# Sparse attention in a two-block kernel: the scores of two heads issued in turn, and two sets of buffers for the turned probabilities

## The reference, cut to what matters

```python
s_s = einsum('bqghd,bgqkd->bghqk', q_b, k_g) + bias_s      # selected
o_s = einsum('bghqk,bgqkd->bqghd', masked_softmax(s_s, mask_s), v_g)
s_w = einsum('bqghd,bkgd->bghqk', q_b, k_w) + head_bias(dist_w)   # window
o_w = einsum('bghqk,bkgd->bqghd', masked_softmax(s_w, mask_w), v_w)
return g_b[..., 0:1] * o_c + g_b[..., 1:2] * o_s + g_b[..., 2:3] * o_w
```

## Time and profile before

| | us |
|---|---|
| median of three runs | 2572.99 (2572.43 to 2579.61) |
| the profiled execution, its own time | 2573.83 |
| its span in the trace | 2572.1 |
| the stage `attend` in it, 2232.3 to 2335.4 | 103.1 |

### The profile page before, as it was taken

One profiled execution on the slowest core, in us unless ns is written; L12 is line 12 of the kernel. 1 busy time (PEld: TensorE's weight loads), 2 busy tenths in 40 slices (PEclk: granted clock), 3 DMA queues, 4 the chain that ended last, 5 costly groups with the idle time before them and its releaser, 6 DMA issues. The chain is left out here.

```text
span 2572.1 us, 38698 instructions
## 1 busy us (share of the span) xinstructions
PE 2339.2 (91%) x15386; PEld 2132.0 (83%) x15386; DVE 1557.1 (61%) x2843; ACT 1131.4 (44%) x1962; POOL 75.0 (3%) x36
## 2 busy tenths in 40 slices
PE   6976779789999999999998998989998999897998
PEld 6964468689999998888887997979997999776997
DVE  5764343479988887666665545665545544565454
ACT  4521233435555444555554444444433443454443
POOL 0121000040100000000000000000000000000000
PEclk9987589899999999999998998999998999788999
DMA  5450033325544444656655555535545554103552
GB/s 202 147 61 10 20 142 117 128 103 173 172 149 148 148 149 148 196 192 194 195 173 199 183 182 197 197 115 211 182 163 200 213 193 166 70 1 118 209 181 98
DMA packets 77854, 388.55 MB, mean 151 GB/s; under 512 B 9707, under 2 KB 12651, under 8 KB 49292
## 3 DMA queue, kind: packets, MB, share of 16 engines
q1 hardware_dynamic: 76380, 382.08, 43.1%
q0 software_dynamic: 1040, 4.19, 1.6%
q10 hardware_dynamic: 288, 0.26, 0.0%
HBM read 381.26 MB, written 5.24 MB: 150 GB/s over the span
## 5 line engine op out<-in xcount | busy, mean ns | idle before, releaser
L243 DVE TENSOR_TENSOR split_slots<-ring,split_slots 128x1024 fp32r<-128x1024 f32 x394 | 464.2, 1224 | 355.3 <-ACT split_slots L234 355.3
L296 PE MATMUL banks<-x_transposed_hi,split_slots 128*128 128x256 f32 x2016 | 581.3, 288 | 44.6 <-PEq L355 39.9
L297 PE MATMUL banks<-x_transposed_lo,split_slots 128*128 128x256 f32 x2016 | 578.9, 287 | 0.0
L298 PE MATMUL banks<-x_transposed_hi,split_slots 128*128 128x256 f32 x2016 | 578.2, 287 | 0.0
L234 ACT ACTIVATE split_slots<-ring 128x1024 fp32r<-128x1024 f32 x404 | 402.5, 1049 | 257.3 <-PE banks L298 224.4
L307 DVE SCALAR_TENSOR_TENSOR expert_lo<-ring,expert_hi 128x512 fp32r<-128x512 f32 x512 | 360.7, 710 | 189.0 <-ACT expert_hi L302 187.9
L302 ACT ACTIVATE expert_hi<-ring 128x512 fp32r<-128x512 f32 x512 | 323.2, 632 | 276.0 <-PE banks L298 275.9
L296 PEld LDWEIGHTS banks<-x_transposed_hi,split_slots 128*128 128x128 f32 x2016 | 395.5, 196 | 49.7 <-issue 42.9
L297 PEld LDWEIGHTS banks<-x_transposed_lo,split_slots 128*128 128x128 f32 x2016 | 395.3, 196 | 1.5
L298 PEld LDWEIGHTS banks<-x_transposed_hi,split_slots 128*128 128x128 f32 x2016 | 395.0, 196 | 0.0
L296 PE MATMUL banks<-x_transposed_hi,expert_hi 128*128 128x256 f32 x1024 | 296.3, 289 | 17.7 <-DVE expert_lo L307 17.2
(11 more groups left out here) (444 smaller groups left out, 3480.8 us busy)
## 6 DMA issues: line engine op xcount, KB each, us to landing
ring<-in_ffn_w SPq DMA_DIRECT2D x132, 1024.0 KB, 4.8
ring<-in_peer_u SPq DMA_DIRECT2D x128, 512.0 KB, 3.3
ring<-in_peer_v SPq DMA_DIRECT2D x128, 512.0 KB, 4.3
ring<-in_w_in SPq DMA_DIRECT2D x16, 1024.0 KB, 4.9
ring<-in_sgu_w_in SPq DMA_DIRECT2D x16, 1024.0 KB, 4.8
ring<-in_peer_wq SPq DMA_DIRECT2D x8, 1024.0 KB, 5.3
ring<-in_sgu_w_out SPq DMA_DIRECT2D x8, 1024.0 KB, 4.8
ring<-in_kv_w SPq DMA_DIRECT2D x6, 1024.0 KB, 5.5
```

Of the source, the lines that this page charges most:

```text
L243: ins = dve.tensor_tensor(self.parts[:, b, 1, p], self.k.w.slot(g)[:, p], self.parts[:, b, 0, p].bitcast(F32), ALU.subtract)
L296: pe.matmul(out, lh, rh, start=start, stop=False)
L297: pe.matmul(out, lh, rl, start=False, stop=False)
L298: return pe.matmul(out, ll, rh, start=False, stop=stop)
```

## The change

The scores of heads `n` and `n+1` are issued together when `n` is even, product by product in turn, so that neighbouring pairs of matmuls belong to different heads. Both wait for the bias additions of both heads of the pair before, and each head's `scored` is counted at its last product. The buffers for the turned probabilities come in two sets, and `copy(h)` waits for `mix(h-2)`.

```diff
-        pT = k.sb(ctx, "probabilities_T", [P, 2, 2, A])
-        pT_last = k.sb(ctx, "probabilities_last_T", [P, 2, A])
-        cT = k.sb(ctx, "cmp_probabilities_T", [16, SEQ])
+        turned_sets = 2
+        pT = [k.sb(ctx, f"probabilities_T_{b}", [P, 2, 2, A]) for b in range(turned_sets)]
+        pT_last = [k.sb(ctx, f"probabilities_last_T_{b}", [P, 2, A]) for b in range(turned_sets)]
+        cT = [k.sb(ctx, f"cmp_probabilities_T_{b}", [16, SEQ]) for b in range(turned_sets)]
...
-        def scores(pe, h):
-            g, p = parts(h)
-            bank = 2 * (h % 2)
-            if h >= 2:
-                pe.wait_ge(biased, 3 * (h - 1))
-            for i, at, n in ((1, bank, B), (0, bank + 1, A)):
-                q = qT[p, h // 2, i * P:(i + 1) * P]
+        def scores(pe, pair):
+            heads = (2 * pair, 2 * pair + 1)
+            if pair >= 1:
+                pe.wait_ge(biased, 3 * heads[0])
+            for i, first_bank, n in ((1, 0, B), (0, 1, A)):
                 for branch, keys in enumerate((s.k_sel, s.k_win)):
-                    pe.matmul(k.psum[:, at, branch * n:(branch + 1) * n], q, keys[p, g, 0:n], start=True, stop=True)
-                ins = pe.matmul(k.psum[:, bank + 1, B + 16 * i:B + 16 * i + NCMP], q, s.k_cmp[p, g, 0:NCMP],
-                                start=True, stop=True)
-            ins.then_inc(scored, 1)
+                    for h in heads:
+                        g, p = parts(h)
+                        pe.matmul(k.psum[:, 2 * (h % 2) + first_bank, branch * n:(branch + 1) * n],
+                                  qT[p, h // 2, i * P:(i + 1) * P], keys[p, g, 0:n], start=True, stop=True)
+                for h in heads:
+                    g, p = parts(h)
+                    ins = pe.matmul(k.psum[:, 2 * (h % 2) + 1, B + 16 * i:B + 16 * i + NCMP],
+                                    qT[p, h // 2, i * P:(i + 1) * P], s.k_cmp[p, g, 0:NCMP], start=True, stop=True)
+                    if i == 0:
+                        ins.then_inc(scored, 1)
...
             for n in range(NH + 3):
-                if n < NH:
-                    scores(pe, n)
+                if n < NH and n % 2 == 0:
+                    scores(pe, n // 2)
...
             def copy(h):
                 act.wait_ge(turned, h + 1)
-                if h >= 1:
-                    act.wait_ge(outs, h)
+                b = h % turned_sets
+                if h >= turned_sets:
+                    act.wait_ge(outs, h - turned_sets + 1)
```

More of the change, by code:

```diff
@@ L2866, in mix @@
             d = slice(g * HDIM, (g + 1) * HDIM)
-            pe.matmul(o[:, 0:SEQ], s.v_cmp[0:NCMP, g, :], cT[0:NCMP, :], start=True, stop=False)
+            pe.matmul(o[:, 0:SEQ], s.v_cmp[0:NCMP, g, :], cT[h % turned_sets][0:NCMP, :], start=True, stop=False)
             for branch, v in enumerate((s.v_sel, s.v_win)):
-                pe.matmul(o[:, 0:SEQ], v[:, 0, d], pT[:, branch, :, :].rearrange("p i t -> p (i t)"), start=False, stop=False)
-                ins = pe.matmul(o[:, A:B], v[:, 1, d], pT_last[:, branch, :], start=False, stop=(branch == 1))
+                pe.matmul(o[:, 0:SEQ], v[:, 0, d], pT[h % turned_sets][:, branch, :, :].rearrange("p i t -> p (i t)"),
+                          start=False, stop=False)
+                ins = pe.matmul(o[:, A:B], v[:, 1, d], pT_last[h % turned_sets][:, branch, :], start=False, stop=(branch == 1))
             ins.then_inc(outs, 1)
@@ L2984, in copy @@
                 act.wait_ge(turned, h + 1)
-                if h >= 1:
-                    act.wait_ge(outs, h)
+                b = h % turned_sets
+                if h >= turned_sets:
+                    act.wait_ge(outs, h - turned_sets + 1)
                 flat = lambda ap: ap.rearrange("p a n -> p (a n)")
-                act.activation(pT[:, :, :, :].rearrange("p a i n -> p (a i n)"), k.psum[:, 4, :], ACT.Copy).then_inc(copied, 1)
-                act.activation(flat(pT_last[:, :, :]), k.psum[:, 5, 0:B], ACT.Copy).then_inc(copied, 1)
-                act.activation(cT[0:NCMP, :], k.psum[0:NCMP, 5, B:2 * B], ACT.Copy).then_inc(copied, 1)
+                act.activation(pT[b][:, :, :, :].rearrange("p a i n -> p (a i n)"), k.psum[:, 4, :], ACT.Copy).then_inc(copied, 1)
+                act.activation(flat(pT_last[b][:, :, :]), k.psum[:, 5, 0:B], ACT.Copy).then_inc(copied, 1)
+                act.activation(cT[b][0:NCMP, :], k.psum[0:NCMP, 5, B:2 * B], ACT.Copy).then_inc(copied, 1)
             def output(j):
```

## The result

The changed kernel takes 2553.58 us (median of 4 runs, 2547.76 to 2555.24) against 2572.78 of before (4 runs, 2572.43 to 2579.61). The ratio is 0.992, with a 95% interval of 0.9896 to 0.9944. In a later set of runs it was 2553.29 against 2570.12: 0.9937, 0.9921 to 0.9953. So it is faster by 0.6 to 0.8%. The forecast had the sign (2561.0) and too little of it; the range ended at 2554, 0.4 us above what was measured.

The account below looks back on a forecast made before the run. TensorE was taken to bound the stage, VectorE next. Start to 25.9 us, five pairs at 9.4, VectorE's step 14 at 4.2 and drain 13.5 gave 90.8 against 103.1, 12.3 less: forecast 2561.0 us, range 2554 to 2580.

Parts of the forecast that it names:

- Part 1: TensorE's scores: matmuls of two heads partly overlap, so a pair takes 4.2 us low clock, 2.3 full.
- Part 2: Pair's scores delay VectorE's step: TensorE waits 1.1 us a pair at full clock; pair 9.4 us in place of 9.8.
- Part 3: Stage start: scores(2,3) wait for head 1's bias, starting at 8.9 us, the first turn following them; loss 2 us.
- The loss that I put at 2 us: Stage start: the first turn now waits for a pair's scores, not only VectorE's step 1; estimated 2 us.
- Part 4: Second buffer set for turned probabilities: no gain or cost in the steady part, drain 13.5 us, 3 less.
- Part 5: TensorE's granted clock: full rows bring the rise, a guess; low clock ends near 24 us into the stage.
- The first such place is mix(0): Full-row stretch expected to raise the clock: mix(0) with what follows, the rise coming as scores(4,5) begin.
- the rival with the full clock almost from the start: Clock rises with the first scores; scores(4,5) end at 18.7 us, not 25.9; 7.2 less, 2554 us; chance 0.08.

Follow-up runs that it names:

- The control on the same rows: The changed kernel with odd heads' scores made from partitions 0 to 63, like even heads', order, waits and buffers kept: 2576.4 us, ratio 1.0021 to the kernel before.

## Why the prediction was wrong, step by step

The signs of the steps held, and two terms of the sum were mis-sized: the scores of a pair, and the time at the low clock. The sum had 90.8 us for the stage, and it took 84.0.

**Part 1, the scores: right in mechanism, mis-sized.** "I take 4.2 and 2.3" was for a pair; it measured 3.53 and 1.86, the lower bound of both. The allowance of 0.7 and 0.4 us "for 24 weight loads and 24 matmuls that one queue has to hand out" came from no row, and nothing of it exists here. Five pairs at the full clock were 0.56 us shorter than forecast (8.88 against 2.3 + 4.1 + 1.02 + 2.02 = 9.44), 2.8 us, four fifths of it by the scores; two at the low clock 0.67 each, 1.3 us. The Trainium skill ("TensorE: Matmul & The Clock Gate", Part 3) has it that matmuls on different row groups run at once, and by that rule a pair would cost one head's time and the stage be some 4 us shorter. The trace agrees: 1.86 us for a pair as for a head. The control on the same rows, 3.61 in place of 1.86, shows that it is the rows. The trace of before had a second crossing that I overlooked, where head 2's first product starts at 2237.76, before head 1's last ones.

**Part 2, the coupling: right.** TensorE waits once a pair, 0.88 us where 1.1 were forecast, and of the 1.86 us that the overlap gives, the full clock keeps 0.9 a pair, where 0.4 of 1.4 were forecast. From scores to turn it was 3.99 us where I had 4.1. That this chain binds is shown by the kernel with `scored` counted twice: 8.33 us a pair.

**Part 3, the start: right.** Scores(2,3) began 8.2 us into the stage; 8.9 was forecast, and the 0.67 of difference is the scores' term again. The loss that I put at 2 us, which is no term of the sum, was smaller: turn(0) began 11.7 us into the stage, against 10.8 before.

**Part 4, the second set: right in the drain, wrong elsewhere.** Alone it gave 3.3 us; 3 was forecast. "It costs and gives nothing there", of the steady part, fails in the new order: with one set a pair took 9.45 and with two 8.88. In the old order it holds: with two sets alone a head still took 4.9 us. The pair order put ScalarE's copy(n-1) behind a mixing that TensorE now reaches late.

**Part 5, the clock: right in direction, mis-sized.** I had it low for 24 us. It was low for 13.6, in three pieces. "The first such place is mix(0)" failed: the clock was up already behind scores(0,1), at 2235.9, when TensorE had done nothing in the stage but 24 matmuls on both halves of the rows. The two later pieces follow on TensorE's own waits. In all, scores(4,5) ended 22.2 us into the stage (2254.81, the next turn) and not at 25.9; 1.3 of these 3.7 are the scores' at the low clock. The rest is for the most part the clock's: turn(1) took 1.03 in place of 1.90, and scores(4,5) 1.90 in place of 2.9, in which the allowance of part 1 stands too. With the 2.8 of the five pairs and 0.3 in the drain (17.4 in place of 17.7) the 6.8 us are accounted for.

The clock is also the larger part of the gain. An estimate: a us at the low clock costs 1 - 4.90 / 9.21 = 0.47 us, and 41.0 - 13.6 = 27.4 us fewer of them are 12.8 of the 19.1 us. With 0.9 us for each of five pairs and the 3.3 of the second set alone the sum is some 20.7; the wait for the bias of head 1 takes some back.

**The range.** Its lower end was the rival with the full clock almost from the start, at 2554, but worked out with scores of 2.3 us. The scores' own lower bound was in the text, worth 4 us, and was not put together with it. The scores reached their bound and the clock came most of the way to the rival, to which I had given a chance of 0.08. The result fell 0.4 us below, and the range should have ended near 2550.

What stays open is how much of the run-to-run spread, 2560 to 2578 us for before in the later sets, comes from the clock in other stages. Time and mean granted clock of an execution go together: of the twelve with one set, the one at 0.945 took 2553.25 us and the one at 0.933 took 2575.55. The stage of the kernel with one set is 9.8 us longer than that of the changed kernel, and yet its profiled execution, 2553.25, was the shorter one: its mean granted clock over the span was 0.945 against 0.941. And why the clock fell in the drain of three experiments (one set, and both with a fill on the kernel before) and in no drain of before was not settled.

## What to carry to other kernels

Where products use half of the array's rows, look whether the next independent product lies on the other half, and put the two next to each other: here two heads cost the time of one. By the estimate above most of what it brought came through the clock, so look at the granted clock of the stage before and after. Then look at what waits for the pair, since issuing two pieces of work as one delays whoever needed the first; counting the semaphore earlier within the pair gave back 0.55 of the 0.94 us a pair that the coupling had taken. And when two unknowns of a forecast have bounds of their own, the range must hold both at the same end.

## What the runs showed of the hardware

- Score products of 64 rows on partitions 0 to 63 and 64 to 127 run fully beside each other, weight loads included: 24 matmuls and 24 weight loads of two heads take 1.86 us (3.53 at the low clock), as the 12 and 12 of one head do. On the same 64 rows they took 3.61.
- Which rows the scores used changed when the granted clock rose. On the same instructions in the same order, 64 rows at a time left it at 0.50 for 41 us with TensorE busy 35.1 of them, and both halves at once had it up 3.4 us after the stage began. The work of one head at a time ran at both levels, in the kernel before at 0.50 for 41.0 us and then at 1.00 for 61.9, so the rows are not the whole of it. The lengths repeated from trace to trace: 41.0 and 41.0 us before, 13.6 and 13.6 changed.
- The clock fell in waits of 3.9 and 4.6 us at the start of the stage, once also behind a wait of 0.79, with TensorE busy 12.36 of the 13.40 us before. Products that nobody reads, put into such waits, carried it through them in three kernels. In two of these it fell a little later all the same (the changed kernel with one fill, and the kernel before with two); in the third, with `scored` counted twice and two fills, it stayed up for 74.2 us, to the stage's end. Where VectorE bound the start, a fill gave nothing: 82.7 us against 82.8.
